# PEER weights stage: one comparison for eight one-hot rows, the weights multiplied in by ScalarE and VectorE, four buffers of rows and four result banks

## The reference

```python
s = einsum('thpd,hpkd->thpk', q, sub_keys)         # scores of 128 + 128 keys a head
s1, i1 = top_k(s[:, :, 0], 16); s2, i2 = top_k(s[:, :, 1], 16)
cand_s = s1[..., :, None] + s2[..., None, :]
cand_i = i1[..., :, None] * 128 + i2[..., None, :]
top_s, pos = top_k(cand_s, 16)                     # 16 experts a head
gate = softmax(top_s)
hid = einsum('td,thkd->thk', x, u_tab[idx])
y = einsum('thk,thkd->td', gelu(hid) * gate, v_tab[idx])
```

## Time and profile before

| | |
|---|---|
| median of three runs | 2732.93 us (2728.82 to 2736.04) |
| the profiled execution | 2727.92 us, its span 2726.1 us |
| busy, share of the span | PE 92%, weight loads 77%, VectorE 70%, ScalarE 48% |
| peer_weights | about 705 to 817 us of the span |

### The profile page before, as it was taken

The page is one execution under the profiler, slowest core; times in us unless marked ns, Lnnn a source line. Parts: engine busy times, 40 slices in busy tenths (PEclk is TensorE's granted clock), DMA queues, the critical chain, the costliest instruction groups (busy, mean ns, idle before and its releaser), DMA issues. The chain is left out here.

```text
span 2726.1 us, 46973 instructions
## 1 busy us (share of the span) xinstructions
PE 2519.2 (92%) x18674; PEld 2106.0 (77%) x18674; DVE 1894.9 (70%) x2918; ACT 1303.6 (48%) x1760; POOL 35.3 (1%) x67
## 2 busy tenths in 40 slices
PE   5999999798789999999999798899999698899997
PEld 3885999764468999999999696678888585788885
DVE  3675676539996666666666666488888665688886
ACT  3553443211234444444444444377776453577775
POOL 1000000000000000000000000000000100000000
PEclk8988999898799999999999899899999799899998
DMA  7235000247675566666666650389998531599994
GB/s 288 93 131 180 3 3 2 99 172 262 218 248 186 186 189 186 185 186 186 189 187 186 251 191 24 124 329 366 364 362 313 225 124 40 209 372 363 364 367 169
DMA packets 132276, 553.72 MB, mean 203 GB/s; under 512 B 11352, under 2 KB 13576, under 8 KB 106776
## 3 DMA queue, kind: packets, MB, share of 16 engines
q1 hardware_dynamic: 127966, 536.00, 54.9%
q0 software_dynamic: 4160, 15.56, 1.7%
HBM read 549.36 MB, written 2.16 MB: 202 GB/s over the span
## 5 line engine op out<-in xcount | busy, mean ns | idle before, releaser
L254 PE MATMUL PS<-over,over 128*128 128x512 f32 (+1 forms) x3040 | 1064.3, 350 | 30.2 <-DVE over L742 8.4
L255 PE MATMUL PS<-over,over 128*128 128x512 f32 (+1 forms) x3040 | 1055.9, 347 | 0.0
L256 PE MATMUL PS<-over,over 128*128 128x512 f32 (+1 forms) x3040 | 1054.6, 347 | 0.0
L254 PEld LDWEIGHTS PS<-over,over 128*128 128x128 f32 x3040 | 584.1, 192 | 100.5 <-issue 17.1
L256 PEld LDWEIGHTS PS<-over,over 128*128 128x128 f32 x3040 | 583.2, 192 | 69.6
L255 PEld LDWEIGHTS PS<-over,over 128*128 128x128 f32 x3040 | 584.0, 192 | 66.4 <-issue 0.5
L3043 DVE TENSOR_TENSOR over<-ring,over 128x2048 fp32r<-128x2048 f32 x240 | 548.8, 2291 | 78.5 <-ACT over L2984 77.4
L2984 ACT CAST over<-ring 128x2048 fp32r<-128x2048 f32 x240 | 457.6, 1914 | 38.1 <-PE PS L256 36.1
L1938 DVE TENSOR_TENSOR over<-ring,over 128x1024 fp32r<-128x1024 f32 x256 | 312.9, 1223 | 107.1 <-ACT over L1934 107.1
L1934 ACT CAST over<-ring 128x1024 fp32r<-128x1024 f32 x256 | 267.7, 1047 | 179.1 <-PE PS L256 174.1
L1947 ACT ACTIVATE ring<-PS 128x256 f32<-128x256 f32 x128 | 49.2, 384 | 232.6 <-PE PS L256 232.6
(11 more groups left out here) (466 smaller groups left out, 2406.6 us busy)
## 6 DMA issues: line engine op xcount, KB each, us to landing
ring<-in_w_gate SPq DMA_DIRECT2D x80, 1024.0 KB, 5.2
ring<-in_w_up SPq DMA_DIRECT2D x80, 1024.0 KB, 7.4
ring<-in_w_down SPq DMA_DIRECT2D x80, 1024.0 KB, 8.1
ring<-in_mod_w SPq DMA_DIRECT2D x64, 1024.0 KB, 5.4
ring<-in_peer_u SPq DMA_DIRECT2D x128, 512.0 KB, 3.5
ring<-in_peer_v SPq DMA_DIRECT2D x128, 512.0 KB, 4.1
ring<-in_w_in SPq DMA_DIRECT2D x12, 2048.0 KB, 8.8
ring<-in_dn_w SPq DMA_DIRECT2D x8, 2048.0 KB, 8.2
```

The lines of the kernel that those rows point to most:

```text
L254: nc.tensor.matmul(out, lhs[0], rhs[0], start=start, stop=False)
L255: nc.tensor.matmul(out, lhs[0], rhs[1], start=False, stop=False)
L256: return nc.tensor.matmul(out, lhs[1], rhs[0], start=False, stop=stop)
```

## The change

VectorE makes the A and the B rows of a group by one comparison, without the gate (`equal`, 128x1024), one group ahead. The gates are then multiplied into the B rows in place: the first `act_rows(n)` of the four, three in even and two in odd groups, by ScalarE (`nc.scalar.activation` with Copy and the gate as its scale), the others by one VectorE multiplication. There are four buffers of rows and four result banks. TensorE waits for both halves of the scaling, and for the bank copy of group n-4. ScalarE scales two groups ahead of its bank copy. VectorE's loop is written out. The chunks' bias moves to words 2048 to 4095 of the ring, which are the third and fourth buffer of `PRAW`, so SP waits for the last chunk's matmuls before it loads the third part of the experts' weights.

```diff
-        hotA = ring[:, 8192:8192 + 1024].rearrange("p (b q k) -> p b q k", b=2, q=GQ)
-        hotB = ring[:, 9216:9216 + 1024].rearrange("p (b q k) -> p b q k", b=2, q=GQ)
+        NHOT = 4
+        hot = ring[:, 8192:12288].rearrange("p (b a q k) -> p b a q k", b=NHOT, a=2, q=GQ)
-        w_bias = ring[0:1, 10240:10240 + CHUNK].rearrange("p (n c) -> p n c", n=GRP)
+        w_bias = ring[0:1, 4096 - CHUNK:4096].rearrange("p (n c) -> p n c", n=GRP)
...
+        def act_rows(n):
+            return 2 if n % 2 else 3
 
         def dve_g(e, c):
-            def body(n, b, first):
-                if not first:
-                    e.wait_ge(s_gmm, n - 1)
-                nc.vector.tensor_tensor(hotA[:, b], bc(iota, 1, GQ), bc(idx[:, 0, bass.ds(n * GQ, GQ)], 2, P),
-                                        ALU.is_equal)
-                for q in range(GQ):
-                    t = n * GQ + q
-                    ins = nc.vector.tensor_scalar(hotB[:, b, q, :], iota, idx[:, 1, bass.ds(t, 1)],
-                                                  idx[:, 2, bass.ds(t, 1)], ALU.is_equal, ALU.mult)
-                ins.then_inc(s_hot, 1)
-            groups_loop(e, body)
+            def equal(n):
+                if n >= NHOT:
+                    e.wait_ge(s_gmm, n - NHOT + 1)
+                nc.vector.tensor_tensor(hot[:, n % NHOT], iota.unsqueeze(1).unsqueeze(1).broadcast_to([P, 2, GQ, P]),
+                                        bc(idx[:, 0:2, n * GQ:n * GQ + GQ], 3, P), ALU.is_equal).then_inc(s_equal, 1)
+
+            def scale(n):
+                at, t = act_rows(n), n * GQ
+                row = hot[:, n % NHOT, 1, at:GQ, :]
+                e.wait_ge(s_equal, n + 1)
+                nc.vector.tensor_tensor(row, row, bc(idx[:, 2, t + at:t + GQ], 2, P), ALU.mult).then_inc(s_scaled, 1)
+            equal(0)
+            for n in range(NGR):
+                if n + 1 < NGR:
+                    equal(n + 1)
+                scale(n)
...
         def pe_g(e, c):
+            for n in range(NGR):
+                e.wait_ge(s_scaled, n + 1)
+                e.wait_ge(s_scaled_a, n + 1)
+                if n >= 4:
+                    e.wait_ge(s_gev, n - 3)
                 for q in range(GQ):
+                    ins = nc.tensor.matmul(PS[:, n % 4, q * NK:(q + 1) * NK], hot[:, n % NHOT, 0, q, :],
+                                           hot[:, n % NHOT, 1, q, :], start=True, stop=True)
...
         def act_g(e, c):
+            def scale(n):
+                e.wait_ge(s_equal, n + 1)
+                for q in range(act_rows(n)):
+                    row = hot[:, n % NHOT, 1, q, :]
+                    ins = nc.scalar.activation(row, row, ACT.Copy, scale=idx[:, 2, n * GQ + q:n * GQ + q + 1])
+                ins.then_inc(s_scaled_a, 1)
+            scale(0)
+            scale(1)
+            for n in range(NGR):
+                if n + 2 < NGR:
+                    scale(n + 2)
                 e.wait_ge(s_gmm, n + 1)
...
             def part(src, n, s, turn):
+                if s == 2:
+                    w_pe.wait(sp, ("l", NG0 * KC - 1))
                 if s >= 4:
                     sp.wait_ge(s_lo, n - 3)
```

More of the change, by code:

```diff
@@ L1763, in build @@
         GQ = 4
-        hotA = ring[:, 8192:8192 + 1024].rearrange("p (b q k) -> p b q k", b=2, q=GQ)
-        hotB = ring[:, 9216:9216 + 1024].rearrange("p (b q k) -> p b q k", b=2, q=GQ)
-        s_hot, s_gmm, s_gev = sem("s_hot"), sem("s_gmm"), sem("s_gev")
-        NG2 = T // GQ // 2
+        NHOT = 4
+        hot = ring[:, 8192:12288].rearrange("p (b a q k) -> p b a q k", b=NHOT, a=2, q=GQ)
+        s_equal, s_scaled, s_scaled_a = sem("g_equal"), sem("g_scaled"), sem("g_scaled_a")
+        s_gmm, s_gev = sem("s_gmm"), sem("s_gev")
+        NGR = T // GQ
         w_buf = [chunk_view(ring[:, 4096 + q * CHUNK:4096 + (q + 1) * CHUNK]) for q in range(2)]
-        w_bias = ring[0:1, 10240:10240 + CHUNK].rearrange("p (n c) -> p n c", n=GRP)
+        w_bias = ring[0:1, 4096 - CHUNK:4096].rearrange("p (n c) -> p n c", n=GRP)
         s_ww, s_wb = [sem(f"w_mod{q}") for q in range(2)], sem("w_bias")
@@ L1787, in build @@
         stream.append(load_w)
[L1789 to L1795, removed]
-        def dve_g(e, c):
-            def body(n, b, first):
-                if not first:
-                    e.wait_ge(s_gmm, n - 1)
-                nc.vector.tensor_tensor(hotA[:, b], bc(iota, 1, GQ), bc(idx[:, 0, bass.ds(n * GQ, GQ)], 2, P),
-                                        ALU.is_equal)
-                for q in range(GQ):
-                    t = n * GQ + q
-                    ins = nc.vector.tensor_scalar(hotB[:, b, q, :], iota, idx[:, 1, bass.ds(t, 1)],
-                                                  idx[:, 2, bass.ds(t, 1)], ALU.is_equal, ALU.mult)
-                ins.then_inc(s_hot, 1)
-            groups_loop(e, body)
+        def act_rows(n):
+            return 2 if n % 2 else 3
+        def dve_g(e, c):
+            def equal(n):
[13 more added lines that the diff above has]
+                scale(n)
             e.wait_ge(s_xhi, 1)
@@ L1815, in pe_g @@
         def pe_g(e, c):
[L1816 to L1819, removed]
+            for n in range(NGR):
[3 more added lines that the diff above has]
+                    e.wait_ge(s_gev, n - 3)
                 for q in range(GQ):
-                    ins = nc.tensor.matmul(PS[:, b, q * NK:(q + 1) * NK], hotA[:, b, q, :], hotB[:, b, q, :],
-                                           start=True, stop=True)
+                    ins = nc.tensor.matmul(PS[:, n % 4, q * NK:(q + 1) * NK], hot[:, n % NHOT, 0, q, :],
+                                           hot[:, n % NHOT, 1, q, :], start=True, stop=True)
                 ins.then_inc(s_gmm, 1)
-            for n in range(2 * NG2):
-                body(n, n % 2, n < 2)
                 for m in w_at.get(n, ()):
@@ L1833, in pe_g @@
                     w_pe.mark(ins, ("l", m))
-            e.wait_ge(s_gmm, 2 * NG2)
+            e.wait_ge(s_gmm, NGR)
             return w_pe
         def act_g(e, c):
-            def body(n, b, first):
+            def scale(n):
[9 more added lines that the diff above has]
+                    scale(n + 2)
                 e.wait_ge(s_gmm, n + 1)
-                nc.scalar.copy(G[:, :, n * GQ:n * GQ + GQ], PS[:, b, :].rearrange("p (q j) -> p j q", q=GQ)).then_inc(s_gev, 1)
-            for n in range(2 * NG2):
-                body(n, n % 2, n < 2)
+                nc.scalar.copy(G[:, :, n * GQ:n * GQ + GQ],
+                               PS[:, n % 4, :].rearrange("p (q j) -> p j q", q=GQ)).then_inc(s_gev, 1)
                 for m in w_at.get(n, ()):
@@ L1846, in act_g @@
                         w_ac.mark(row_copy(e, NG0 + m // KC), ("row", m // KC))
-                if n == NG2:
+                if n == NGR // 2:
                     e.wait_ge(s_px, 16)
                     nc.scalar.copy(xs_hi, hT).then_inc(s_xhi, 1)
-                if n == 2 * NG2 - 3:
+                if n == NGR - 3:
                     w_pe.wait(e, ("l", NG0 * KC - 1))
                     peer_hi(e, 0, 0)
-            e.wait_ge(s_gev, 2 * NG2)
+            e.wait_ge(s_gev, NGR)
             e.wait_ge(s_xhi, 1)
```

## The result

The changed kernel takes 2710.21 us (median; 2705.29 to 2715.58), the kernel before 2732.50 us beside it: 22.3 us less, a ratio of 0.9918 with a 95% interval of 0.9902 to 0.9935. The profiled execution took 2707.38 us, with a span of 2705.6 us. The forecast was 2713.1 us.

The account below looks back on a forecast made before the run. VectorE was taken to bound the weights stage: 90.3 us of work plus 1.5 of stalls, 91.8 against 111.6, 19.8 us less; 2727.92 became 2708.1, plus 5.0 for the median 2713.1 us, range 2704 to 2726.

Parts of the forecast that it names:

- What bounds the stage: Weights stage: VectorE bounds it at 1.64 us a group, 111.6 us with 6 us of waits.
- The term of each instruction: VectorE per group: 1.14 us for the new comparison, 0.20 or 0.34 for the scaling, 1.41 on the mean.
- The stalls: VectorE's waits in the weights stage: 1.5 us in all, bounds 0 and 6; 6 us before.
- TensorE's sum of 88.5 us: TensorE's groups, chunks and bias products in the weights stage: 88.5 us, 1.36 us a group.
- the prediction's signs of being wrong: Weights stage: comparisons further apart without a wait, TensorE waiting for in_mod_w, or a clock under 1.00.
- the rival: Granted clock falls in the weights stage, slower beyond 23 us of TensorE work at half clock; 2754 us, shared slower chance 0.04.
- another engine: Another engine or the loads hold the weights stage: gain 11 to 15 us, 2720 us; chance 0.17.
- The loads: Chunk loads in the weights stage: 1.25 to 1.37 us a group, transfer share 0.89, fits barely, nothing booked.
- The end: Tail after VectorE's last group: stays 3.5 us, delayed third peer transfer hidden at zero, at most 0.4 us once.
- The sum: Weights stage: 91.8 us against 111.6, 19.8 us less, giving a median of 2713.1 us.
- the upper bound: VectorE's part if scaling waits for its comparison: 0.12 us more a group, 98.0 us instead of 90.3.
- The rule: Fast fp32 tensor_scalar, two results a cycle, would make the change lose 17 us; removed instructions were said not to get it.

Follow-up runs that it names:

- b_buffers: The kernel before with four row buffers and four result banks, loop, bias and SP's wait as in the change; 2719.63 us beside 2729.87, ratio 0.9960.
- a_small: The changed kernel with the chunks' products over 64 columns instead of 512; stage body 89.9 us against 92.0.
- a_act3: The changed kernel with ScalarE scaling three rows in every group and VectorE one; stage body 93.0 us against 92.0.
- a_act4: The changed kernel with all four rows scaled by ScalarE, none by VectorE; stage body 104.7 us, end 7.4 us.
- a_small3: The changed kernel with ScalarE scaling three rows in every group and the chunks' products over 64 columns instead of 512; stage body 89.0 us.
- a_early: The changed kernel with every chunk of the modulation vectors two groups earlier; 2709.21 us beside 2729.87, ratio 0.9923, end 3.68 us.
- a_bias: The changed kernel with the bias product at the fifth chunk of each eight, so peer loads wait for chunk 20, not 23; end 4.82 us against 5.98.
- a_split: The changed kernel with the comparison of eight rows made by two 128x512 instructions; stage body 94.3 us against 92.0.
- a_chain: The changed kernel with VectorE's scaling right behind its own comparison instead of one comparison later; stage body 97.9 us against 92.0.
- b_onescalar: The kernel before with the B rows' TENSOR_SCALARs comparing only, one scalar from a tile instead of two; stage body 104.8 us against 111.6.
- b_immediate: The kernel before with constants in place of both scalars of the B rows' TENSOR_SCALARs; stage body 101.3 us against 111.6.
- a_hot2: The changed kernel with two buffers of rows instead of four, four result banks kept; 2809.85 us, stage body 197.6 us.

## Why the prediction was right

**What bounds the stage.** Right: in b_buffers VectorE holds the old work alone, and a_small gives VectorE's part of the new as 89.9 us, forecast 90.3. That it bounds the changed kernel alone is not so, see below. The term of each instruction held: 1.14 for the comparison, 0.20 and 0.34 for the scaling (1.33 and 1.47 us between comparisons).

**The stalls.** 1.8 us measured (1.5 of them waits for TensorE), 1.5 forecast. The parts were not as forecast and offset each other, which is luck too: VectorE waited 0.5 and 0.7 us after the first two bias products where 0.3 each was booked, 0.3 us behind the conversion where nothing was, and 0.3 us at the start where 0.9 was. And what stands behind them was undersized. TensorE's sum of 88.5 us was for the full clock. In the stage it is busy 85.7 of the 87 us from 710 to 797, with the granted clock at 0.50 at its start:

```profile
710.00:715.00 5.00, 4.66 (x22) 4.69 (x23) 5.00 (x9) 3.72 (x11) 0.00 (x0) 0.50 0.29 120
```

A clock under 1.00 in the stage was one of the prediction's signs of being wrong. It came, but the rival priced it from 23 us of TensorE's work at half clock on; here it was 5 us, from TensorE's first product at 710.3 us to 715.6 us. So TensorE is as full as VectorE, and the four buffers hide that from the body's length. The rival "another engine" did not come to pass, but it stood close by: a_act3 took 4.5 us off VectorE's work and got nothing.

**ScalarE.** 0.29 us for an ACTIVATE, 1.65 us a group with four rows (a_act4): right. The conversion made TensorE 0.6 us late, 0.7 forecast, and most of that was covered by the slack, as said; a_small3 shows it uncovered.

**The loads.** The transfer share is 0.89 to 0.96 where 0.89 was worked out. Loads land after 5.1 to 5.9 us, and TensorE's matmuls waited for them 0.2 us, its weight loads 0.7. Right for the changed kernel; with three rows for ScalarE these waits grew (1.2 us in a_act3), so the loads were not far behind either.

**The end.** Wrong by 2.4 us: it was booked at zero. The step that failed is "The new wait holds back the third peer transfer (and the fourth in SP's queue) until that chunk is done ... I take it as hidden, at zero". Its timing was off: the bias product, put at 0.9 us before VectorE is through, ended at 800.2, 0.6 us after, and SP issued the third transfer at 800.3 and not 0.8 us before the tail. But the third load was still in time. I followed the loads to ScalarE, who wants them, and found cover. I did not follow POOL's store of the last modulation row, which waits for the same chunk, is queued with these loads, and is waited for at the barrier. a_early and a_bias show it.

**The sum.** Forecast 19.8 us for body and end, measured 17.2 in the traces: 19.6 less 2.4. The medians lie 22.3 us apart, with an interval of 17.8 to 26.8 us, so 17.2 lies just outside of it. That the median came within 3 us of the forecast is in part luck: what was missed at the end came back, and more, from stages for which the forecast booked nothing. In the kernel before the next stage begins at half clock, in the changed one at full:

```profile
806.00:812.00 6.00, 6.00 (x51) 5.91 (x50) 4.93 (x7) 5.48 (x8) 0.00 (x0) 1.00 0.58 197
```

The prediction had put 3 us on this, either way. The rest of the program, from that first product on, is the same work in all fourteen kernels. In the five whose granted clock over its first 3 us was 0.50 to 0.68 (before, a_split, a_act3, a_chain, b_onescalar) it took 1904.2 to 1905.8 us, in the nine at 1.00 it took 1898.2 to 1903.5. So the 5.8 us between the two traces go with that half clock. What decides it is not shown: b_onescalar and b_immediate have the same end, 3.57 us, and are one of each kind, and a_split, close to the changed kernel, is of the other kind than it. One trace of each kernel can't tell how often the change brings the full clock. The stage's start moves too, from 703.8 to 709.8 us over the fourteen, with nothing ahead of it changed.

**The waits of the rivals.** That the scaling might have to wait out its comparison was the upper bound, 0.12 us a group; a_chain shows that this is the price when the order is not looked ahead, and that it is not paid in the changed kernel.

**The rule.** I said that the removed instructions do not get the fast form because they took 0.26 us. Their price was right, the reason wrong: they do, and pay for their scalars. The sum didn't rest on it.

## What to carry to other kernels

Take work off the bounding engine and give buffers in one step: here the buffers alone brought 7.5 us, 16 us less of VectorE's work alone 7, the buffers with 15 us less of it (105 to 90.2) 19.6. When a stage is compressed, follow every transfer that waits for the same event up to the barrier, small stores too: here the store landed behind the loads issued before it. And look at the second engine before making the first one lighter still: with VectorE and TensorE both full, 4.5 us less for VectorE gave nothing.

## What the runs showed of the hardware

- A wait for the VectorE instruction just ahead costs 0.12 us (1.25 us from its start against 1.13); with one other instruction in between it costs nothing (a_chain against the changed kernel).
- Each scalar from a tile costs a VectorE TENSOR_SCALAR 0.06 us, on 128x128 f32 (0.135, 0.195, 0.26 us from one to the next for none, one, two; b_immediate, b_onescalar, before).
- Where TensorE waited for rows at nearly every group, the granted clock was 0.77 on the mean of 198 us (a_hot2), and groups that take 2.75 us at full clock took 3.09 on the mean.
- An 8 KB store took 1.7 us when the 512 KB load ahead of it was 1.4 us from landing, and 4.0 and 4.4 us when it was 3.9 and 4.2 us away; in all fourteen kernels it landed 0.1 to 0.4 us after that load, though POOL issues it and SP the loads.
